# Four fp32 output projections of a hybrid decoder step as 2x2 block products with seven products each, by halves of the tokens

## The reference, cut to what matters

```python
# layer 0: gated DeltaNet mixer, layer 1: sparse attention mixer; each then a SwiGLU FFN
for i in range(2):
    h  = rmsnorm(x, norm1_w[i])
    x  = x + mixer_i(h)            # ends in  o @ w_out      (1088 x 1024) @ (1024 x 1024)
    x  = x + swiglu_ffn(rmsnorm(x, norm2_w[i]), ffn_w_in[i], ffn_w_out[i])
y = rmsnorm(x, final_norm_w)

def swiglu_ffn(x, w_in, w_out):
    g, u = jnp.split(x @ w_in, 2, axis=-1)
    return (jax.nn.silu(g) * u) @ w_out    # (1088 x 2816) @ (2816 x 1024)
```

## Time and profile before

| | |
|---|---|
| three runs | 4315.81, 4316.61, 4322.1 us; median 4316.61 |
| profiled execution | 4315.64 us, of which the span of its instructions is 4314.0 us |
| PE busy | 3978.2 us, 92% of the span |
| DVE, ACT, POOL busy | 1413.9, 890.6 and 860.2 us |
| granted TensorE clock, mean | 0.961 of 2.4 GHz |
| time of the GDN out stage on PE | from 1212.69 us to 1334.17 us |
| time of the FFN0 out stage on PE | from 1911.63 us to 2238.00 us |

### The profile page before, as it was taken

One profiled execution on the slowest core, in us unless ns is written; L12 is line 12 of the kernel. 1 busy time (PEld: TensorE's weight loads), 2 busy tenths in 40 slices (PEclk: granted clock), 3 DMA queues, 4 the chain that ended last, 5 costly groups with the idle time before them and its releaser, 6 DMA issues. The chain is left out here.

```text
span 4314.0 us, 52988 instructions
## 1 busy us (share of the span) xinstructions
PE 3978.2 (92%) x19902; PEld 2882.3 (67%) x19902; DVE 1413.9 (33%) x2750; ACT 890.6 (21%) x1952; POOL 860.2 (20%) x786
## 2 busy tenths in 40 slices
PE   5799999998799999999999968998989999999999
PEld 4466666666656888876656746666655688887665
DVE  3256555455524111110020024666652411111002
ACT  1232333332211000000000003565541100000001
POOL 0011111111101332310000003566640133321000
PEclk7899999999789999999999889999999999999999
DMA  1201111110022111121111130000021211112101
GB/s 58 87 26 40 35 35 30 35 40 20 11 84 86 39 39 39 39 88 40 28 29 34 58 107 1 1 1 2 1 75 39 78 46 39 39 39 88 40 27 55
DMA packets 257221, 183.23 MB, mean 42 GB/s; under 512 B 26266, under 2 KB 249491, under 8 KB 256083
## 3 DMA queue, kind: packets, MB, share of 16 engines
q1 hardware_dynamic: 251590, 174.68, 13.8%
q0 software_dynamic: 2048, 5.25, 0.4%
q10 hardware_dynamic: 3456, 1.57, 0.2%
HBM read 155.63 MB, written 29.91 MB: 43 GB/s over the span
## 5 line engine op out<-in xcount | busy, mean ns | idle before, releaser
L276 PE MATMUL ps<-work 128*128 128x363 f32 (+1 forms) x2184 | 671.5, 471 | 7.4 <-DVEq L372 7.4
L520 PE MATMUL ps<-xT,work 128*128 128x272 f32 x2688 | 643.5, 393 | 0.0
L276 PEld LDWEIGHTS ps<-work 128*128 128x128 f32 x2184 | 416.8, 191 | 261.5 <-DVEq L372 8.5
L520 PEld LDWEIGHTS ps<-xT,work 128*128 128x128 f32 x2688 | 512.4, 191 | 104.0
L1004 PE MATMUL ps<-xn,work 128*128 128x363 f32 (+1 forms) x1536 | 550.7, 478 | 24.2 <-DMA work<-in_gdn_w_in_dram 17.6
L520 PE MATMUL ps<-xn,work 128*128 128x272 f32 x2016 | 491.7, 394 | 3.9 <-DVE work L593 3.9
L520 PEld LDWEIGHTS ps<-xn,work 128*128 128x128 f32 x2016 | 384.9, 191 | 83.2 <-issue 5.1
L2368 POOL TENSOR_SCALAR work<-work 128x640 f32<-128x640 f32 (+4 forms) x192 | 313.6, 1643 | 197.0 <-DVE work L2271 196.7
L1004 PEld LDWEIGHTS ps<-xn,work 128*128 128x128 f32 x1536 | 263.1, 193 | 121.5 <-issue 37.5
L276 PE MATMUL ps<-xn,work 128*128 128x363 f32 (+1 forms) x1056 | 324.3, 470 | 6.3 <-DMA work<-in_nsa_w_out_dram 6.3
L276 PEld LDWEIGHTS ps<-xn,work 128*128 128x128 f32 x1056 | 201.2, 191 | 128.7 <-issue 7.9
(11 more groups left out here) (358 smaller groups left out, 4509.4 us busy)
## 6 DMA issues: line engine op xcount, KB each, us to landing
work<-in_ffn_w_in_dram SPq DMA_DIRECT2D x88, 512.0 KB, 5.0
work<-in_ffn_w_out_dram SPq DMA_DIRECT2D x16, 1408.0 KB, 7.0
work<-in_gdn_w_in_dram SPq DMA_DIRECT2D x32, 512.0 KB, 4.2
ffn_parked_residual<-xT SPq DMA_DIRECT2D x2, 4352.0 KB, 12.8
xT<-ffn_parked_residual SPq DMA_DIRECT2D x2, 4352.0 KB, 13.9
out_dram<-work SPq DMA_DIRECT2D x9, 512.0 KB, 2.6
parked_residual<-xT SPq DMA_DIRECT2D x1, 4352.0 KB, 12.7
xT<-gate_rows SPq DMA_DIRECT2D x8, 544.0 KB, 4.2
```

The source lines that it names most:

```text
L276: mm = pe.matmul(a, w[:, k, :], rhs[:, k, o:o + n], start=(k == 0), stop=(k == nk - 1))
L520: ins = pe.matmul(acc(a, n), w[:, k, :], t[:, k, a * SUB:(a + 1) * SUB], start=(first and k == 0), stop=(k == HK - 1), skip_group_check=True)
```

## The change

`out_stage` no longer goes tile by tile over all tokens, but in eight steps. Steps 0 to 3 treat the first 544 tokens and steps 4 to 7 the last 544; a step treats a pair of output k-tiles (two rows of blocks), the two halves of the inner features (`lo`, `hi`, nk/2 k-tiles each) and two blocks of 272 tokens. The 2x2 by 2x2 block product is made of seven products (`product1` to `product7`) of nk/2 matmuls of 272 columns instead of eight. For that,

- four token combinations a step are made on DVE, each of nk/2 x 272 columns (`mix1`, `mix2`, and the ones that set `t4` and `t3`), in two buffers `tx` and `ty`;
- four weight combinations a step are made on POOL (on DVE for the first step), each of nk/2 x 128 columns;
- the weights of a step are loaded in four parts ("roles": gl, ul, uh, gh, each nk/2 x 128), and loaded once for each half of the tokens, so twice;
- DVE adds the products in PSUM to the residual and to `pu`, and POOL adds `pu` to three of the four blocks;
- ACT copies product 1, and squares each block of 272 columns; POOL adds the squares to `p.ssq`.

The norm goes by halves of 544 tokens: the first half is summed in step 5, its reciprocal taken in step 6 and its rows normalised in step 7. The second half is left to the next stage (`second_half`), in which `mm_first` now treats chunk 0 of both first tiles, then sums, then chunks 1 and 2 of both. Around it: one `recycle_semaphores` is added between the GDN stage and FFN0, the first weights of the attention stage are loaded to another place, the weight buffers of the FFN's out stage and `tx` lie in `c.xn`, and the residual comes back in two parts (`back0`, `back1`).

```diff
+    FIRST, LATER = (1, 5, 2, 4, 3, 7, 6), (1, 2, 4, 5, 3, 7, 6)      # order of the products
@@ SP
+                for n in range(1, STEPS):
+                    sp.wait_ge(pd, done(n - 1, 1))
...
+                    ow.load(sp, src, n, 0)
+                    sp.wait_ge(s2, n)
+                    sp.wait_ge(pd, done(n - 1, 4))
+                    ow.load(sp, src, n, 1)
+                    sp.wait_ge(pd, done(n - 1, 5))
+                    sp.wait_ge(s4, n)
+                    ow.load(sp, src, n, 2)
+                    sp.wait_ge(pd, done(n - 1, 6))
+                    ow.load(sp, src, n, 3)
@@ PE
+                def product(n, a, w, t, first):
+                    for k in range(hk):
+                        mm = pe.matmul(acc(n, a), w[:, k, :], t[:, k, :], start=(first and k == 0), stop=(k == hk - 1), skip_group_check=True)
+                    mm.then_inc(pd, 1)
...
+                    def product2():
+                        pe.wait_ge(s2, n + 1)
+                        pe.wait_ge(t2, n + 1)
...
+                        product(n, 1, w2, ty, True)
...
+                    def product3():
+                        pe.wait_ge(s3, n + 1)
+                        pe.wait_ge(t3, n + 1)
...
+                        product(n, 2, ul, tx, True)
@@ DVE
+                for n in range(STEPS):
+                    dve.wait_ge(cp, n + 1)
+                    dve.wait_ge(pd, done(n, 2))
+                    dve.tensor_tensor(pu, pu, acc(n, 1), ALU.add).then_inc(u2, 1)
+                    dve.wait_ge(t2, n + 1)
+                    dve.tensor_tensor(ty, rhs[:, hi, tokens(n, 0)], ty, ALU.subtract).then_inc(t4, 1)
+                    dve.wait_ge(pd, done(n, 4))
+                    dve.wait_ge(pa, 3 * n + 1)
+                    dve.tensor_tensor(x(n, 1, 1), x(n, 1, 1), acc(n, 3), ALU.add).then_inc(x22a, 1)
+                    dve.tensor_tensor(tx, rhs[:, hi, tokens(n, 1)], rhs[:, lo, tokens(n, 1)], ALU.subtract).then_inc(t3, 1)
...
+                    if n == STEPS - 2:
+                        dve.wait_ge(root, 1)
+                        inverse(c, dve, p, 0).then_inc(inv, 1)
...
+                        for k in range(KD // 2):
+                            normalise(c, dve, p, 0, k).then_inc(nrm, 1)
@@ POOL
+                for n in range(STEPS):
...
+                    pool.wait_ge(u2, n + 1)
+                    for row, half in ((1, 1), (0, 1), (1, 0)):
+                        pool.tensor_tensor(x(n, row, half), x(n, row, half), pu, ALU.add).then_inc(pa, 1)
+                    pool.wait_ge(ow.gh, 16 * npc * (n + 1))
+                    pool.wait_ge(s2, n + 1)
+                    pool.wait_ge(pd, done(n, 2))
+                    pool.tensor_tensor(w2, gh, w2, ALU.subtract).then_inc(s4, 1)
+                    add_squares(n, 1)
...
+                        pool.wait_ge(pd, done(n, 3))
+                        pool.wait_ge(ow.ul, 16 * npc * (n + 2))
+                        pool.wait_ge(ow.uh, 16 * npc * (n + 2))
+                        pool.tensor_tensor(w1, ul, uh, ALU.add).then_inc(s1, 1)
+                    add_squares(n, 2)
...
+                        pool.tensor_tensor(w2, w1, gl, ALU.subtract).then_inc(s2, 1)
+                        pool.tensor_tensor(ul, gl, ul, ALU.subtract).then_inc(s3, 1)
+                    if not last_pair:
+                        add_squares(n, 3)
+                        add_squares(n, 4)
@@ the first tiles of the next stage
+def mm_first(c, pe, p, tiles, normed, summed):
+    for dst, w, done in tiles:
+        o, n = CH[0]
+        for k in range(KD):
+            pe.matmul(dst[0], w[:, k, :], c.xn[:, k, o:o + n], start=(k == 0), stop=(k == KD - 1))
+    square_sum(c, pe, p, 1, 6).then_inc(summed, 1)
+    for dst, w, done in tiles:
+        for (o, n), a in zip(CH[1:], dst[1:]):
+            for k in range(KD):
+                pe.wait_ge(normed, k + 1)
+                mm = pe.matmul(a, w[:, k, :], c.xn[:, k, o:o + n], start=(k == 0), stop=(k == KD - 1))
+        mm.then_inc(done, 1)
```

More of the change, by code:

```diff
@@ L322, in out_stage, with inverse, normalise @@
[L322 to L326 removed]
+HT = NT // 2
+SUB = HT // 2
+def inverse(c, dve, p, half):
+    o = half * HT
+    return dve.reciprocal(p.sq[:, o:o + HT], p.sq[:, o:o + HT])
+def normalise(c, dve, p, half, k):
+    o = half * HT
+    return dve.scalar_tensor_tensor(out=c.xn[:, k, o:o + HT], in0=c.xT[:, k, o:o + HT], scalar=c.normw[:, p.which * 8 + k:p.which * 8 + k + 1],
+                                    in1=p.sq[:, o:o + HT], op0=ALU.mult, op1=ALU.mult)
@@ new lines, in square_sum, with root_of @@
+def square_sum(c, pe, p, half, b):
+    for n in range(2):
+        o = half * HT + n * SUB
+        pe.matmul(bank(c, b + n)[:, 0:SUB], const(c, "ones"), p.ssq[:, o:o + SUB], start=True, stop=False)
+        mm = pe.matmul(bank(c, b + n)[:, 0:SUB], const(c, "ones"), p.sq[:, o:o + SUB], start=False, stop=True)
+    return mm
+def root_of(c, act, p, half, b):
+    o = half * HT
+    return act.activation(p.sq[:, o:o + HT].rearrange("p (n t) -> p n t", n=2), bank(c, b, 2).rearrange("p (n t) -> p n t", n=2)[:, :, 0:SUB],
+                          ACT.Sqrt, bias=const(c, "eps"), scale=1.0 / D)
@@ new lines, in out_stage, with done, acc, tokens @@
+def out_stage(c, ow, src, npc, rhs, loaded, p, after=None, back=None):
+    nc = c.nc
+    hk = ow.hk
+    STEPS, PAIRS = 8, 4
+    FIRST, LATER = (1, 5, 2, 4, 3, 7, 6), (1, 2, 4, 5, 3, 7, 6)
+    lo, hi = slice(0, hk), slice(hk, 2 * hk)
+    pu, tx, ty = ow.pu, ow.tx, ow.ty
+    def done(n, product):
+        return 7 * n + (LATER if n else FIRST).index(product) + 1
+    def acc(n, a):
+        return bank(c, 4 * (n % 2) + a)[:, 0:SUB]
+    def tokens(n, half):
+        o = (n // PAIRS) * HT + half * SUB
+        return slice(o, o + SUB)
+    def x(n, row, half):
+        return c.xT[:, 2 * (n % PAIRS) + row, tokens(n, half)]
+    def added_by(n, which):
+        return sum(2 if m % PAIRS == PAIRS - 1 else 4 for m in range(n)) + which
@@ L327, in out_stage @@
     with ExitStack() as ctx:
[L328 to L331, removed]
+        pd, cp, u2, x11, x22a, x22b, x12, x21, t1, t2, t3, t4, s1, s2, s3, s4, pa, sqd, added, summed, root, inv, nrm = sems(
+            nc, ctx, c, "product_done", "product1_copied", "sum2_ready", "row11_done", "row22_part", "row22_done", "row12_done", "row21_done",
+            "tokens1_mixed", "tokens2_mixed", "tokens3_mixed", "tokens4_mixed", "weights1_mixed", "weights2_mixed", "weights3_mixed",
+            "weights4_mixed", "sum2_added", "rows_squared", "squares_added", "squares_summed", "rooted", "inverted", "normed")
@@ L334, in _ @@
             def _(sp):
[L335 to L344, removed]
+                for role in range(4):
+                    if role not in loaded:
+                        ow.load(sp, src, 0, role)
@@ L421 @@
 HK = KD // 2
-HT = NT // 2
-SUB = HT // 2
 def ffn_buffers(c):
```

369 lines of the change are left out of this document (221 added, 148 removed).

## The result

The changed kernel takes 4354.41 us (median of four runs, 4351.18 to 4355.16) against 4318.03 of the kernel before beside it (4315.81 to 4322.1): ratio 1.0082, 95% interval 1.0064 to 1.0099. It is slower by 36 us, outside the predicted range of 4278 to 4341. The profiled execution took 4353.97 us with a span of 4352.2, which is 38.2 more than the 4314.0 before.

A forecast was written before the change was run, and what follows sets the result against it. PE, busy for 92% of the span, was taken to bound the kernel. The terms -109 - 2.4 + 53 + 11 + 6 + 28 + 13 gave -0.4 us on a span of 4314.0, rounded to 4314; range 4278 to 4341.

The forecast's parts named there:

- part 2: GDN, NSA and FFN steps: two-SBUF-input DVE operations and POOL's do not overlap; GDN and NSA +26.5 us each, FFN steps fit.
- Theory P: FFN out stages, from the experiments: PE waits because `mix2` loses the port to `s3`; seven waits of 2.5 us each stage.
- Rival C: GDN and NSA ring longer than counted, deciding from 16.9 us a step; FFN overrun by 1 us, +16 more; 4340; chance 0.23.
- Columns: Out stages: fewer PE columns, -40.0 us in each FFN and -14.5 in each of GDN and NSA, -109 together.
- the sign: GDN and NSA out stages: PE busy at some 75 to 80% in the new profile.
- Step 0 of the FFNs: FFN out stages' first step: product 2 +1, product 5 waits 0.7, product 3 +4; 5.7 us each, +11 together.
- Product 2's +1: FFN's first step: product 2 waits for DVE's combinations, 11.4 us against 10.1 of products 1 and 5, with hand-overs +1.
- The ring of GDN and NSA: GDN and NSA out stages: hand-overs from one product 2 to the next take 16.4 us, PE idling 3.6 in each.
- Handing over: Behind GDN and NSA: 6.2 us between PE's records, +3.9 and +2; FFNs 0; +6 in all.
- The norm's second half: Three stage beginnings: PE idles 5.5 us behind the sum, then 0.7; with 12.9 us of slow clock, +28.
- Clock inside the steps: Slow PE stretches behind gaps: 9.5 us in GDN and NSA, 3.4 in the FFNs, +13 together.

The follow-up runs named there:

- the kernel with the yield: The changed kernel with POOL waiting for DVE's `mix2` of the next step (`t2`) before its last weight combination `s3`: 4307.45 us.
- two edits of one line each: Against the changed kernel: `s3` held until the next step's token sum (`t2`), 4307.45 us; `s3` held only until POOL's own `s2` ended, 4312.53 us.
- the third, 26 us: The changed kernel with only POOL's addition of squares behind `s3` held until the next step's token sum (`t2`): 4328.72 us.
- the last two experiments on these stages: GDN and NSA without POOL's additions of squares, on the `t2` wait before `s3`: 4293.75 us; with a seventh weight buffer, on that wait plus two-part norm: 4268.74 us.
- the split: The changed kernel with the norm's second half summed, rooted, inverted and normalised in two parts, 544 to 725 and 726 to 1087: 4305.2 us.
- the third experiment: The changed kernel with the out stages of GDN and NSA taken from the kernel before, the new ones in the FFNs only: 4289.82 us.

## Why the prediction was wrong

The forecast was 4314 us and no change; measured were 4354. The step that failed is in part 2, on the FFN steps: "31.1 against 35.3 of PE. That fits, and the order of waits leaves each combination a product's length (5.04 us) to hide in." The load was right and it fits: the kernel with the yield puts the same work through the port, and there the stage takes 293.4 us. What does not follow from it is that each combination finds the port free in time. `mix2` has one product's length, 5.04 us, less some 0.5 for the addition ahead of it (L556), for its 3.27, so a margin of 1.3; waiting for `s3` costs 3.1 and for the square 0.8 more, and the excess is the gap: 0.5 + 6.37 - 5.04 = 1.8 and 0.5 + 7.1 - 5.04 = 2.56, as measured. I summed the port over a step and never wrote out who stands beside whom, as I had done for GDN. I had also read from the earlier trace rows that the later one waits. Those rows show a case against it: POOL's operation began at 233.02, DVE's L1357 at 233.17, and it was POOL that waited. Theory P is shown by two edits of one line each, 47 and 42 us; the third, 26 us, shows it only in part, since 10.3 of the 16.6 us of waits that it saved come from steps in which DVE won against `s3` without the edit's doing.

With the yield alone the kernel is at 4307, 7 us below the forecast. So this wait, with the clock behind it, is more than the whole miss, and the rest was predicted somewhat too dear: GDN and NSA at 29 us each for 19.7 and 25.2 measured.

Rival C's sign for the FFNs, gaps inside their steps, did come. Its reason was another one, POOL overrunning PE's step ("if it overran by 1 us, +16 more"); POOL was in time here, and DVE's combination stood behind it. The mechanism that rival C counted on, a ring of more than 16.9 us in GDN and NSA, did not come.

By the other steps:

- **Columns.** With the waits gone PE's busy time in FFN0's out stage is 288.8 us against 326.4 before, -37.6 for a predicted -40; 295.6 in the changed kernel, with the lower clock. In GDN and NSA it is 111.9 and 113.5 instead of some 121.4, -9.6 and -7.9 where the columns alone give -14.5; the clock (below) is part of that, the rest I did not separate. PE was busy for 88% and 84% of the two windows, where 75 to 80% was to be the sign. Roughly right.
- **Step 0 of the FFNs.** Predicted 0.7 and 4 us, measured 0.58 and 4.02. Product 2's +1 did not show. Right.
- **The ring of GDN and NSA.** Predicted 16.4 us in both. NSA 16.3, right, and its stage is 134.6 us for 121.4, +13.2 against +12. GDN 15.6, 0.8 less; a 256 KB part landed in 2.8 us there (median), not in the 3.6 that I took from the earlier trace rows, which fits, but no run separates it; 127.6 for 121.5, +6.1 against +12. That uh's load and an addition of squares lie in the ring, and that the port's sum does not set it, is shown by the last two experiments on these stages.
- **Handing over.** 6.24 us behind GDN and 6.10 behind NSA for a predicted 6.2. Right.
- **The norm's second half.** Gaps of 5.21 us at all three beginnings for a predicted 5.5, and 9.6 and 10.1 us more than before from the first matmul to the pairs, for 10.2 and 9.2. Right; taking them away by the split shows the cause.
- **Clock inside the steps.** In the FFNs three slow stretches of 1.7 us a stage came on top of the one predicted, all behind waits that I had not predicted. In GDN and NSA the granted clock was 0.97 and 0.96 over the stages, against 0.99 in GDN's before. If the lower level is half of the upper, 0.97 over 127.6 us is 7.7 us at the lower one, of which half is lost; worked out so for both, and less the 1.2 us of before each, 7 us for the 9.5 that I took. Right in size.
- **Not predicted:** the gap before the FFN out stages grew from 2.46 to 4.27 and 4.40 us. SP now issues four loads there before the end of the block; that this is the reason was only argued.

Still open: what tips the port when `s3` stands directly behind `s2`. `s3` won in all twelve such steps of the changed kernel, in eight of twelve with the wait before the squares, and in ten of twelve with the split norm, with no change between the two instructions. So both outcomes occur in one execution, and the 34 us between the runs of the third experiment may be the same race; no profile shows it. The wait on `s2` alone did control it: `mix2` won in all twelve.

## What to carry to other kernels

A resource that two engines share must be laid out in time and not only summed. Ask for each operation that PE waits for which of the other engine's operations can be in the way, back to back, and what its margin is; an unhurried one of them belongs behind a wait. Where two engines race for it, count the outcome over all steps of a profile before an edit is given the credit. One such line was worth 1.1% here, and an experiment on one wait may well pay for another, since shorter waits of PE also keep its clock up. Fewer products pay where a step is long: 5.0 us a product hid DVE's and POOL's sums in the FFNs, 1.8 us in GDN and NSA did not.

## What the runs showed of the hardware

- When a POOL operation ends and a DVE operation has been waiting for the port, POOL's next one can still go first if it stands directly behind with no wait of its own: `mix2` began at 2095.47, `s3` at 2095.53, and `s3` went first. This was so in all twelve such steps of the changed kernel, in ten of twelve with the split norm and in eight of twelve with the wait before the squares. The recorded starts do not tell the cases apart: `mix2` had begun 0.04 to 0.15 us before `s2` ended where it lost, and 0.06 to 0.12 where it won. With a wait on POOL's own predecessor between the two, `s3` came 0.22 us after `mix2` began, and `mix2` went first in twelve of twelve. The Trainium skill says in "SBUF — State Buffer", Who interferes with whom, that the order of issue decides who blocks. The trace agrees in the steps with that wait, also in the two where `s3` began 0.2 us ahead and won. It does not agree where one engine's instructions stand back to back: there the later start mostly won.
- DVE did the same before the change. Its L1357, directly behind L1426, went ahead of a POOL operation that had begun 0.15 us earlier; L1358, directly behind L1357, did not.

```profile
232.56 0.68 DVE L1426 TENSOR_TENSOR work<-work,xT 128x512 f32<-128x512 f32 x1
```

- Where the following instruction has a wait that is long fulfilled, as the addition of squares has behind `s3`, it went both ways: ahead of `mix2` in all twelve such steps of the changed kernel, behind it in all ten of the split norm's profile, with no change in that stage.
- Behind gaps of 2.54 to 2.61 us the next 22 records took 6.97 us in four steps of the changed kernel and 5.28 in six; behind 2.16 us, 6.97 in both; behind gaps of 1.38 to 1.83 us, 5.28 in all ten of the profile with the wait before the squares.
